# The output stage of a hybrid attention and mixture-of-experts block: routing work inside the next tile's product, and the root by Ln and Exp

## The reference

```
x   = x + gate1 * (merged @ w_out)
h2  = RMSNorm(x) * (1 + scale2) + shift2
logits = h2 @ w_router + b_router            # 32 experts
top_vals, top_idx = top_k(logits, 4); weights = softmax(top_vals)
# assignments sorted by expert into blocks; each expert computes a clamped SwiGLU FFN on its tokens
x   = x + gate2 * sum_k weights_k * expert_k(h2)
out = RMSNorm(x)
```

## Time and profile before

| | |
|---|---|
| median of 3 runs | 2820.94 us (2815.48 to 2822.08) |
| span of the profiled execution | 2818.7 us |
| output stage, first product to the next stage | 862.8 to 1005.25 us |
| route stage | 1005.25 to 1036.1 us |
| PE, DVE, ACT, POOL busy over the span | 92%, 71%, 58%, 15% |
| mean granted TensorE clock | 0.952 |

### The profile page before, as it was taken

How to read it: one execution, slowest core, us unless ns; L and a number is a source line. 1 busy time by engine, 2 the same in 40 slices (tenths; PEclk the granted TensorE clock), 3 DMA queues, 4 the chain that set the end, 5 groups by cost and what they waited for, 6 DMA issues and landing times. The chain is left out here.

```text
span 2818.7 us, 41633 instructions
## 1 busy us (share of the span) xinstructions
PE 2594.6 (92%) x12249; PEld 2092.8 (74%) x12249; DVE 1992.5 (71%) x2809; ACT 1630.3 (58%) x2347; POOL 415.2 (15%) x515
## 2 busy tenths in 40 slices
PE   4999899996798939999998999999999999999994
PEld 4888667775686837777776888888888888888881
DVE  4333044543555667666666899999999999999995
ACT  5221144342343236555565788888888888888882
POOL 0000010101000230111111111111111111112110
PEclk7999999997899959999999999999999999999995
DMA  5753222211335357766777899999999999999975
GB/s 212 262 186 109 73 83 88 75 49 58 114 127 172 113 200 274 247 230 222 259 261 266 326 375 375 380 381 373 379 379 375 377 377 378 377 371 372 381 291 196
DMA packets 156202, 714.72 MB, mean 254 GB/s; under 512 B 22988, under 2 KB 43390, under 8 KB 91492
## 3 DMA queue, kind: packets, MB, share of 16 engines
q1 hardware_dynamic: 128304, 636.63, 58.9%
q0 software_dynamic: 26608, 72.98, 9.7%
q10 hardware_dynamic: 1220, 4.21, 0.4%
HBM read 658.04 MB, written 64.73 MB: 256 GB/s over the span
## 5 line engine op out<-in xcount | busy, mean ns | idle before, releaser
L2068 DVE TENSOR_TENSOR e_gu_lo<-gu_raw,e_gu_hi 128x1024 fp32r<-128x1024 f32 x676 | 800.6, 1219 | 70.7 <-ACT e_gu_hi L2064 64.8
L2064 ACT ACTIVATE e_gu_hi<-gu_raw 128x1024 fp32r<-128x1024 f32 x676 | 681.0, 1055 | 10.6 <-PE e_pgu L85 8.5
L83 PE MATMUL e_pgu<-e_gu_hi,e_x_hi 128*128 128x512 f32 x1344 | 547.5, 407 | 5.1 <-issue 5.1
L85 PE MATMUL e_pgu<-e_gu_hi,e_x_lo 128*128 128x512 f32 x1344 | 528.0, 393 | 0.0
L84 PE MATMUL e_pgu<-e_gu_lo,e_x_hi 128*128 128x512 f32 x1344 | 526.8, 392 | 0.0
L2638 DVE TENSOR_TENSOR e_dn_lo<-dn_raw,e_dn_hi 128x1024 fp32r<-128x1024 f32 x336 | 398.3, 1220 | 20.0 <-ACT e_dn_hi L2456 19.8
L2456 ACT ACTIVATE e_dn_hi<-dn_raw 128x1024 fp32r<-128x1024 f32 x336 | 344.5, 1056 | 4.6 <-PE e_pdn L2366 2.8
L85 PEld LDWEIGHTS e_pgu<-e_gu_hi,e_x_lo 128*128 128x128 f32 x1344 | 253.0, 188 | 54.7
L83 PEld LDWEIGHTS e_pgu<-e_gu_hi,e_x_hi 128*128 128x128 f32 x1344 | 254.3, 189 | 44.5 <-issue 5.5
L84 PEld LDWEIGHTS e_pgu<-e_gu_lo,e_x_hi 128*128 128x128 f32 x1344 | 254.3, 189 | 39.8
L83 PE MATMUL e_pdn<-e_dn_hi,e_a_hi 128*128 128x512 f32 x672 | 266.6, 397 | 5.9 <-DVE e_a_lo L2681 5.9
(11 more groups left out here) (440 smaller groups left out, 4496.3 us busy)
## 6 DMA issues: line engine op xcount, KB each, us to landing
gu_raw<-in_w_gate_up_dram SPq DMA_DIRECT2D x336, 1024.0 KB
dn_raw<-in_w_down_dram SPq DMA_DIRECT2D x168, 1024.0 KB, 9.1
wada_later<-in_w_ada_dram SPq DMA_DIRECT2D x32, 512.0 KB
win_raw<-in_w_in_dram POOLq DMA_DIRECT2D x5, 2048.0 KB
proj_by_token<-out_stage SPq DMA_DIRECT2D x32, 256.0 KB, 2.0
wg_raw<-in_w_in_dram POOLq DMA_DIRECT2D x16, 512.0 KB, 4.4
gates_transposed<-g_stage POOLq DMA_DIRECT2D x32, 256.0 KB
gate_in<-gates_transposed SPq DMA_DIRECT2D x16, 512.0 KB
```

Of the source, the lines that this page charges most:

```text
L83: pe.matmul(out, a[0], w[0], start=first, stop=False)
L85: return pe.matmul(out, a[1], w[0], start=False, stop=last)
L2064: act.activation(m.gu_hi[:, b, 2 * j:2 * j + 2], m.gu_raw[:, b, 2 * j:2 * j + 2].rearrange("p k g n -> p k (g n)"), ACT.Copy).then_inc(m.g ...
L2068: dve.tensor_tensor(m.gu_lo[:, b, 2 * j:2 * j + 2], m.gu_raw[:, b, 2 * j:2 * j + 2].rearrange("p k g n -> p k (g n)"), m.gu_hi[:, b, 2 * j ...
```

## The change

TensorE's `route` is taken apart. Within `product(t)`, at k = 3 of the second half, the transposes of h2 of tile t - 1 are issued; at k = 6 of the second half, the ranks of t - 2 and the router product of t - 1. VectorE does the logits of t - 1 and the slots and kept weights of t - 2 between x2 and h2. The root and its reciprocal become Ln and then Exp with scale -0.5, both on ScalarE. Tile 6 is listed at the end of the output stage and no longer in the route stage, and the last router product stands behind the ranks of tile 6. GpSimd no longer waits for the lists at the end of the stage; the semaphores live on into the next one. In the route stage, clearing `xg` goes from GpSimd to ScalarE (a Copy with scale 0), and so does the increment of the bias (from VectorE, as Identity with a bias of one); clearing `pick` comes ahead of the lists.

```
+TURN_H_K, LOGIT_K = 3, 6
-        LISTED = NT - 2
+        LISTED = NT - 1
 # ScalarE
-                act.activation(nrm[:, t, 1:2], nrm[:, t, 0:1], ACT.Sqrt, scale=1.0 / D, bias=m.eps[:, 0:1]).then_inc(rooted, 1)
+                act.activation(nrm[:, t, 1:2], nrm[:, t, 0:1], ACT.Ln, scale=1.0 / D, bias=m.eps[:, 0:1]).then_inc(logged, 1)
+                act.wait_ge(logged, t + 1)
+                act.activation(nrm[:, t, 2:3], nrm[:, t, 1:2], ACT.Exp, scale=-0.5).then_inc(rstd, 1)
 # GpSimd, end of the output stage
-            for b in range(2):
-                pool.wait_ge(r.listed[b], 16 * TOPK * ((LISTED + 1 - b) // 2))
 # VectorE
-                dve.wait_ge(rooted, t + 1)
-                dve.reciprocal(nrm[:, t, 2:3], nrm[:, t, 1:2]).then_inc(rstd, 1)
+                if t:
+                    logits(t - 1)
+                if t >= 2:
+                    find_slots(dve, v, m, r, t - 2, t - 2)
+                    keep_weights(dve, m, r, t - 2, t - 2)
                 dve.wait_ge(rstd, t + 1)
                 ... h2 in two passes ...
                 if t:
-                    logits(t - 1)
-                if t >= 2:
-                    find_slots(dve, v, m, r, t - 2, t - 2)
-                    keep_weights(dve, m, r, t - 2, t - 2)
-                if t:
                     select_experts(dve, v, m, r, t - 1, t - 1)
                     weigh_experts(dve, v, m, r, t - 1, t - 1)
-            logits(NT - 1)
             find_slots(dve, v, m, r, NT - 2, NT - 2)
             keep_weights(dve, m, r, NT - 2, NT - 2)
+            logits(NT - 1)
 # TensorE, in product(t)
                 for half, k in order:
+                    if t and (half, k) == (1, TURN_H_K):
+                        turn_h(t - 1)
+                    if t and (half, k) == (1, LOGIT_K):
+                        if t >= 2:
+                            rank(t - 2)
+                        score(t - 1)
 # TensorE, the order
-            for t in range(NT + 1):
-                if t < NT:
-                    product(t)
-                if 2 <= t < NT:
+            for t in range(NT):
+                product(t)
+                if t >= 2:
                     turn_weights(pe, m, r, t - 2, t - 2)
-                if t:
-                    route(t - 1)
+            turn_h(NT - 1)
+            rank(NT - 2)
             turn_weights(pe, m, r, NT - 2, NT - 2)
+            pe.wait_ge(r.rank_kept, NT - 1)
+            score(NT - 1)
 # route stage, GpSimd
-            for k in range(TOPK):
-                pool.indirect_dma_start(... tile 6's entries ...)
+            pool.memset(m.pick[:].bitcast(F32), 0.0)
             list_tokens(pool, m, r, LAST, 0)
-            pool.memset(m.pick[:].bitcast(F32), 0.0)
-            pool.memset(m.xg[:], 0.0).then_inc(xg_set, 1)
             for b in range(2):
-                pool.wait_ge(r.listed[b], 16 * TOPK)
+                pool.wait_ge(r.listed[b], 16 * TOPK * NT // 2)
 # route stage, ScalarE
+            act.activation(m.xg[:]..., m.eps[:].to_broadcast([P, SLOTS * D]), ACT.Copy, scale=0.0).then_inc(xg_set, 1)
+            act.wait_ge(bias_raw, 64)
+            act.activation(braw[2 * NE:P], braw[2 * NE:P], ACT.Identity, bias=m.ones[2 * NE:P, 0:1]).then_inc(bias_up, 1)
 # route stage, VectorE
-            dve.wait_ge(bias_raw, 64)
-            dve.tensor_scalar(braw[2 * NE:P], braw[2 * NE:P], 1.0, None, ALU.add).then_inc(bias_up, 1)
```

More of the change, by code:

```diff
@@ L1527, in routing_tiles @@
     r.slots = sem(name + "_slots")
-    r.listed = [sem(name + f"_listed{i}") for i in range(2)]
+    r.listed = m.listed
     r.wc_out = sem(name + "_wc_out")
@@ L1589, in find_slots @@
     v.step(dve.scalar_tensor_tensor(out=r.slot[:, b], in0=r.idf[:, b, 0:TOPK], scalar=float(LIST), in1=r.slot[:, b], op0=ALU.mult, op1=ALU.add))
-    if n >= 2:
-        dve.wait_ge(r.listed[b], 16 * TOPK * (n // 2))
+    if t >= 2:
+        dve.wait_ge(r.listed[b], 16 * TOPK * (t // 2))
     dve.tensor_copy(r.slotu[:, b], r.slot[:, b]).then_inc(r.slots, 1)
@@ L1669, in phase_out @@
         sumsq = sem("o_sumsq")
-        rooted = sem("o_rooted")
+        logged = sem("o_logged")
         rstd = sem("o_rstd")
@@ L1820, in product, with turn_h @@
                 ins.then_inc(unit, 1)
-            def route(t):
+            def turn_h(t):
                 pe.wait_ge(h2_done, t + 1)
@@ L1825, in route @@
                     pe.wait_ge(h2T_done, t)
-                    pe.wait_ge(logit_out, t)
                 else:
@@ L1831, in route, with score @@
                 ins.then_inc(turned, 1)
+            def score(t):
                 if t:
-                    rank_tokens(pe, m, r, t - 1, t - 1)
+                    pe.wait_ge(logit_out, t)
                 pe.wait_ge(h2T_done, t + 1)
@@ L1839, in route, with rank @@
                 ins.then_inc(logit, 1)
-            for t in range(NT + 1):
-                if t < NT:
-                    product(t)
-                if 2 <= t < NT:
+            def rank(t):
+                pe.wait_ge(logit_out, t + 1)
+                rank_tokens(pe, m, r, t, t)
+            for t in range(NT):
+                product(t)
+                if t >= 2:
                     turn_weights(pe, m, r, t - 2, t - 2)
-                if t:
-                    route(t - 1)
+            turn_h(NT - 1)
+            rank(NT - 2)
             turn_weights(pe, m, r, NT - 2, NT - 2)
+            pe.wait_ge(r.rank_kept, NT - 1)
+            score(NT - 1)
 def phase_route(nc, m):
@@ L1861, in phase_route @@
         r = routing_tiles(m, ctx, "r")
-        LAST, BEFORE = NT - 1, NT - 2
+        LAST = NT - 1
         cnt = sb(ctx, "r_cnt", [NE, 8], F32)
@@ L1914, in _ @@
             pool.dma_start(m.rows[0:1, 0, 0:1].bitcast(F32), m.h2[0:1, 0:1]).then_inc(m.scattered, 16)
-            for k in range(TOPK):
-                pool.indirect_dma_start(out=m.lists[:, :], out_offset=bass.IndirectOffsetOnAxis(ap=m.slotu[:, BEFORE % 2, k:k + 1], axis=0),
-                                        in_=m.entry[:, k, BEFORE, :], in_offset=None).then_inc(r.listed[BEFORE % 2], 16)
+            pool.memset(m.pick[:].bitcast(F32), 0.0)
             list_tokens(pool, m, r, LAST, 0)
-            pool.memset(m.pick[:].bitcast(F32), 0.0)
-            pool.memset(m.xg[:], 0.0).then_inc(xg_set, 1)
             for b in range(2):
-                pool.wait_ge(r.listed[b], 16 * TOPK)
+                pool.wait_ge(r.listed[b], 16 * TOPK * NT // 2)
             pool.wait_ge(m.scattered, 16)
@@ L1933, in _ @@
             act.activation(r.sh[:, LAST % 2], r.sh[:, LAST % 2], ACT.Exp).then_inc(r.exped, 1)
+            act.activation(m.xg[:].rearrange("p s n -> p (s n)"), m.eps[:].to_broadcast([P, SLOTS * D]), ACT.Copy, scale=0.0).then_inc(xg_set, 1)
+            act.wait_ge(bias_raw, 64)
+            act.activation(braw[2 * NE:P], braw[2 * NE:P], ACT.Identity, bias=m.ones[2 * NE:P, 0:1]).then_inc(bias_up, 1)
             act.wait_ge(bias_up, 1)
@@ L2934, in build @@
             m.slotu = right("slots", [P, 2, TOPK], U32)
+            m.listed = [nc.alloc_semaphore(f"listed{i}") for i in range(2)]
             m.so_far = right("tokens_so_far", [P, NT, NE], F32)
@@ L2958, in build @@
             end_phase()
-            phase_sems.extend(kept)
+            phase_sems.extend(kept + m.listed)
             routing.close()
```

## The result

The changed kernel takes 2831.85 us (median of 6 runs, 2827.64 to 2838.48) against 2820.07 for the kernel before (6 runs, 2815.48 to 2823.51). The ratio is 1.0043, with a 95% interval of 1.0026 to 1.0060: slower by 12 us. The forecast was 2827, no difference by its own limit of 0.3%, with a range of 2814 to 2835.

The account below looks back on a forecast made before the run. The prediction took TensorE to bound the output stage. Its terms, +6.2 for the periods, +0.5 clock, +1.7 tail and -2.2 route stage, gave +6.2 us on the median 2820.94: 2827, range 2814 to 2835.

Parts of the forecast that it names:

- The deciding term: Norm's root in the output stage: Ln and Exp each load a table, so h2 is ready 1.33 us later.
- that rival: One table serves Ln and Exp, so h2 is done before TensorE asks; total 2810 us, chance 0.08.
- I count 0.5 for the whole stage; bounds 0 and 7 x 1.6: Output stage, TensorE: time lost to the lower clock after the change, 0.5 us in all.
- a slow stretch that falls before the transposes only eats idle time: Output stage, TensorE: lower-clock matmuls ahead of the transposes only use up the 2.07 us wait for h2.
- Rival 2: The lower clock stays, slowing the six matmuls that end the product, 1.2 us each, seven times; 2835 us, chance 0.17.
- The tail: From the last product's end to the route stage: 21.3 us, +1.7, with POOL's scatters the last work before the barrier.
- The upper bound of 4: Upper limit on the tail's growth, some +4 us, if the barrier also waits for the scatters to land.
- The route stage: Stage behind the tail: ends 2.2 us sooner, bounds 0.8 and 3.2, as scatters start earlier and VectorE gets time back.
- 6.2: Output stage: with periods of 16.3 us the last product ends 6 to 6.5 us later, taken as +6.2.
- "slower" at 0.29: Chance of a slower result: rival 2's 0.17 in large part and the upper fifth of the prediction's own case.

Follow-up runs that it names:

- The filled run: The changed kernel with nine needless matmuls put into TensorE's idle time before the transposes of tiles 0 to 6: 2827.86 us, ratio 1.0028.
- the run with the two passes alone: The kernel before with only the clearing of the gathered rows and the bias increment moved to ScalarE in the route stage: 2818.74 us, ratio 0.9992.

## Why the prediction was right and where it was off

**The deciding term was right.** Ln and Exp each load a table, 8 and 8 in the stage; h2 comes 9.45 behind the product's end (9.42 reckoned), TensorE stands about 2 us, and the undisturbed period is 16.23 to 16.27 (16.3). The run with Sqrt shows the reverse side: periods of 14.9 from tile 3 on. The rule that one load serves both, "ScalarE: Activation LUTs" in the Trainium skill, section on table sets, was held against the earlier trace rows, and the rows were right: that rival's 2810 needed it.

**The clock was mis-sized.** The term "I count 0.5 for the whole stage; bounds 0 and 7 x 1.6" measured 6.3 to 6.4: four stretches at the lower level, 1.6 each. The step behind it that failed is "a slow stretch that falls before the transposes only eats idle time". The stretches did not fall there. They began with or just behind the restart, on the transposes and the nine matmuls behind them, where nothing absorbs them. Its premise failed with it: the prediction took the light stretches as harmless for being shorter than the 3.2 us of before, and a standing still of 1.9 to 2.6 us was followed by a slow stretch in four periods. Each of the three kernels that share this order of TensorE (products 119.6 to 119.7) has four such periods. Rival 2 had the mechanism, the standing still of 2 us, in its argument, but put the stretch on the last six matmuls; its 2835 lay nearer to the measured 2831.85 than my 2827. The filled run takes this term away (119.6 to 113.3).

**The tail was under-sized.** +1.7 was reckoned, +3.8 measured. The order within it was right: slots at 1006.56, E + 14.8 (15.05), last scatter over at E + 19.9 (20.1), logits in its shadow. What was missing is the barrier behind it: I took 1.23, it was 3.5. The upper bound of 4 covered it; its reason, a barrier that waits until the scatters have landed, fits in size but isn't shown. The run that lists tile 6 late takes 4.8 from the tail and gives 2.2 back in the route stage, so that this part of the change is itself a loss of 2.6 in these two profiles.

**The route stage was right, its exact size by luck.** -2.2 reckoned, -2.1 measured, with the 2.5 back on VectorE and the scatters 2.1 nearer the stage's start; GpSimd and not VectorE ends it, as reckoned, and the run with the two passes alone gains 0.3. But the entries took 1.8 longer to arrive than before, a wait that the prediction held constant, and the same code took 29.2 to 30.6 in other profiles; the forecast could as well have missed by 1.

**The sum.** With the measured clock, tail and route stage it is 6.2 + 6.3 + 3.8 - 2.1 = 14.2, which is what the stages show (12.5 + 3.8 - 2.1); between the medians lie 11.8. Both stood in the range, in the part given to "slower" at 0.29; I had held "same" to be twice as likely because the two mis-sized terms each stood at the low side of their bounds.

## What to carry to other kernels

When work is moved forward into a stream that never waited, compare the time at which it will be asked for with the time at which its input is ready; here the second table load of 1.3 us a tile cost 0.3 to 0.5 where h2 had six microseconds to spare (and that through VectorE's queue), and its full 1.3 where it had none. A wait on TensorE is to be priced with the clock that it can take along: 2 us of standing still brought 1.6 more in four of seven periods. Thin work set behind the product's end rather than inside it gave h2 that time back and was worth 20 us.

## What the runs showed that was not expected

Nine needless matmuls made the kernel faster than it was with the same time spent idle (products 113.3 against 119.6): the clock stayed at 1.00 in all seven periods. And a barrier right behind GpSimd's indirect transfers takes 3.5 us after the last one is issued, against 1.2 behind VectorE's work; the explicit wait for their landing came on top of that with only 1.3.

Standing still is not the only thing that brings the clock down. In the kernel before TensorE stood only 0.86 us a tile, but between the ranks and the router product, and four of five periods were at 0.90. With the same ranks and router product and no idle time beside them, behind the product or inside it, the clock stayed at 1.00 in each of these periods in three kernels. It isn't settled by this order alone either: the kernel before with Ln and Exp stood 0.86 to 1.3 us at the same place in each tile, and only one of its last five periods was at 0.90. What decides between two periods with the same work is open.
